# Weight loads of a four-layer decoder trunk: two pairs of row blocks (1 MB) at a time, into one buffer of eight pairs that the remainders overwrite

## The reference

```python
for i in range(DEPTH):                      # 4; x is (1, 256, 2048)
    hn = rmsnorm(x, norm_g[i])
    if kind == 0:   y = diff_attention(hn, da_w_in[j], da_w_out[j], ...)   # w_in 2048 x 8192
    elif kind == 1: y = sliding_window_attention(hn, sw_w_in[j], ...)      # w_in 2048 x 4608
    else:           y = mlstm(hn, ml_w_in[j], ..., ml_w_out[j], ...)       # w_in 2048 x 8208
    x = x + y
return rmsnorm(x, final_g)
# inside each mixer
proj = h @ w_in
...
return (o * silu(g)) @ w_out               # w_out 2048 x 2048
```

## Time and profile before

| | us |
|---|---|
| time, median of 3 runs | 1760.14 |
| lowest and highest | 1760.11, 1761.57 |
| the profiled execution, its own time | 1759.14 |
| its span, first to last instruction | 1757.4 |
| PE busy | 1747.9 |
| DVE busy | 1142.0 |
| ACT busy | 908.9 |

### The profile page before, as it was taken

One profiled execution on the slowest core, in us unless ns is written; L12 is line 12 of the kernel. 1 busy time (PEld: TensorE's weight loads), 2 busy tenths in 40 slices (PEclk: granted clock), 3 DMA queues, 4 the chain that ended last, 5 costly groups with the idle time before them and its releaser, 6 DMA issues.

```text
span 1757.4 us, 25060 instructions
## 1 busy us (share of the span) xinstructions
PE 1747.9 (99%) x8278; PEld 1459.6 (83%) x8278; DVE 1142.0 (65%) x1900; ACT 908.9 (52%) x1420; POOL 38.0 (2%) x99
## 2 busy tenths in 40 slices
PE   9999999999999999999999999999999999999998
PEld 7888888888888888888888888888888888888887
DVE  6766766665658888855656455655666666666655
ACT  7454545454546666655544445444545445454543
POOL 1000000000000000000000000000000000000000
PEclk9999999999999999999999999999999999999999
DMA  8565565555565554556997699855565656556564
GB/s 252 179 188 177 171 188 166 181 174 184 186 189 165 156 154 140 172 179 165 161 165 200 186 162 181 212 173 190 181 184 163 182 178 182 177 179 179 167 215 144
DMA packets 171012, 313.16 MB, mean 178 GB/s; under 512 B 10838, under 2 KB 27804, under 8 KB 170812
## 3 DMA queue, kind: packets, MB, share of 16 engines
q1 hardware_dynamic: 170512, 311.02, 62.9%
q10 hardware_dynamic: 380, 1.08, 0.2%
q0 software_dynamic: 48, 0.13, 0.1%
HBM read 310.10 MB, written 2.10 MB: 178 GB/s over the span
## 4 chain that ended last, share of the span: by engine, by line
PE 98%; issue 1%; DVE 0%; ACT 0%; DMA 0%; SPq 0%; POOLq 0%; POOL 0%; DVEq 0%; ACTq 0%
PE acc L944 30%; PE acc L946 30%; PE acc L945 30%; PE tp L909 4%; PE sc L945 1%; PE sc L946 1%; PE sc L944 1%; PE sc L976 0%; DMA xres<-in_x_dram 0%; PE sc L1030 0%; PE sc L1032 0%; ACT w_hi L881 0%; PE sc L1031 0%; PE sc L1014 0%; PE sc L1013 0%
## 5 line engine op out<-in xcount | busy, mean ns | idle before, releaser
L1755 DVE TENSOR_TENSOR w_lo<-raw,w_hi 128x1024 fp32r<-128x1024 f32 x583 | 708.2, 1223 | 468.1 <-ACT w_hi L881 466.9
L881 ACT ACTIVATE w_hi<-raw 128x1024 fp32r<-128x1024 f32 x583 | 613.4, 1058 | 467.4 <-PE acc L946 415.2
L944 PE MATMUL acc<-w_hi,xt_hi 128*128 128x512 f32 x1824 | 720.5, 395 | 0.0
L946 PE MATMUL acc<-w_hi,xt_lo 128*128 128x512 f32 x1824 | 711.8, 390 | 0.0
L945 PE MATMUL acc<-w_lo,xt_hi 128*128 128x512 f32 x1824 | 710.6, 390 | 0.0
L946 PEld LDWEIGHTS acc<-w_hi,xt_lo 128*128 128x128 f32 x1824 | 342.6, 188 | 73.0
L945 PEld LDWEIGHTS acc<-w_lo,xt_hi 128*128 128x128 f32 x1824 | 343.2, 188 | 65.9
L944 PEld LDWEIGHTS acc<-w_hi,xt_hi 128*128 128x128 f32 x1824 | 342.9, 188 | 65.5
L944 PE MATMUL acc<-w_hi,ot_hi 128*128 128x512 f32 (+1 forms) x520 | 202.7, 390 | 0.0
L946 PE MATMUL acc<-w_hi,ot_lo 128*128 128x512 f32 (+1 forms) x520 | 201.0, 387 | 0.0
L945 PE MATMUL acc<-w_lo,ot_hi 128*128 128x512 f32 (+1 forms) x520 | 200.6, 386 | 0.0
(11 more groups left out here) (286 smaller groups left out, 1136.3 us busy)
## 6 DMA issues: line engine op xcount, KB each, us to landing
raw<-in_da_w_in_dram SPq DMA_DIRECT2D x255, 512.0 KB, 3.8
raw<-in_ml_w_in_dram SPq DMA_DIRECT2D x96, 512.0 KB, 5.4
raw<-in_sw_w_in_dram SPq DMA_DIRECT2D x72, 512.0 KB, 3.8
raw<-in_da_w_out_dram SPq DMA_DIRECT2D x64, 512.0 KB, 4.3
raw<-in_sw_w_out_dram SPq DMA_DIRECT2D x32, 512.0 KB, 4.0
raw<-in_ml_w_in_dram SPq DMA_DIRECT2D x64, 256.0 KB, 4.7
raw<-in_ml_w_out_dram SPq DMA_DIRECT2D x32, 512.0 KB, 4.6
xres<-in_x_dram SPq DMA_DIRECT2D x3, 512.0 KB, 10.0
```

Of the source, the lines that this page charges most:

```text
L881: act.activation(w_hi[:, q:q + 2, :], raw[:, q:q + 2, :], ACT.Copy).then_inc(hi_ready, 1)
L944: pe.matmul(out_ap, k_hi, m_hi, start=start, stop=False)
L946: return pe.matmul(out_ap, k_lo, m_hi, start=False, stop=stop)
L1755: dve.tensor_tensor(w_lo[:, q:q + 2, :], raw[:, q:q + 2, :], w_hi[:, q:q + 2, :].bitcast(F32), ALU.subtract).then_inc(lo_ready, 1)
```

## The change

Raw weights and remainders share one buffer of 16 chunks, a whole job. `raw` is placed, its place is given back, and `w_lo` is put at the same address: DVE's subtraction now writes over the raw weights that it reads. `w_hi` stays a ring of four pairs. In SBUF this takes as much as before: 16 + 8 chunks in place of three times 8.

SP loads two pairs (four chunks, 1 MB) with one transfer. It waits for PE instead of DVE: the transfer for pairs P and P+1 goes out when PE is through with pair P-7, the second of the two pairs that lie in the same place. For the "ml" job q and k there are two transfers of 512 KB, one for each column stripe, as before two of 256 KB. ACT waits for a landing at even pairs only. In the first job the weights still come by single pairs, now with no wait for any slot, and the parts of `x` stand elsewhere among them.

```diff
@@ buffers @@
-        raw = sb("raw", [P, RING, JW])
-        w_hi, w_lo = sb("w_hi", [P, RING, JW], F32R), sb("w_lo", [P, RING, JW], F32R)
+
+        with ExitStack() as place:
+            raw = place.enter_context(nc.sbuf_tensor("raw", [P, KC, JW], F32))
+        w_lo = sb("w_lo", [P, KC, JW], F32R)
+        w_hi = sb("w_hi", [P, RING, JW], F32R)
@@ semaphores @@
-        raw_full = [sem(f"raw_full{s}") for s in range(4)]
-        raw_half = [sem(f"raw_half{s}") for s in range(4)]
+        raw_full = [sem(f"raw_full{s}") for s in range(PAIRS)]
+        raw_half = [sem(f"raw_half{s}") for s in range(PAIRS)]
@@ load_first @@
-                    for n in {2: (1,), 4: (2, 3)}.get(p, ()):
-                        load_x(n)
+                    if p in (2, 3, 5):
+                        load_x((p + 1) // 2)
                     if p == LAG:
                         load_small()
-                    s = p % LAG
-                    if p >= LAG:
-                        sp.wait_ge(lo_ready, p + 1 - LAG)
+                    s = p
@@ load_out @@
-                for q in range(len(OUT_ORDER)):
+                for q in range(0, len(OUT_ORDER), 2):
                     n, p = OUT_ORDER[q]
-                    s = q % LAG
-                    sp.wait_ge(lo_ready, PAIRS * OUT0[l] + q + 1 - LAG)
...
+                    assert OUT_ORDER[q + 1] == (n, p + 1)
+                    s = q % PAIRS
+                    sp.wait_ge(pairs_done, PAIRS * (OUT0[l] - 1) + q + 2)
...
@@ load @@
-                for p in range(PAIRS):
-                    s = p % LAG
-                    sp.wait_ge(lo_ready, PAIRS * J + p + 1 - LAG)
-                    rows_of = w[P * 2 * p:P * 2 * p + 2 * P, :].rearrange("(k p) n -> p k n", p=P)
+                for p in range(0, PAIRS, 2):
+                    s = p
+                    sp.wait_ge(pairs_done, PAIRS * J + p + 2 - PAIRS)
+                    rows_of = w[P * 2 * p:P * 2 * p + 4 * P, :].rearrange("(k p) n -> p k n", p=P)
                     if pair_of:
...
-                            sp.dma_start(raw[:, 2 * s:2 * s + 2, half * a:half * a + half],
+                            sp.dma_start(raw[:, 2 * s:2 * s + 4, half * a:half * a + half],
...
-                        sp.dma_start(raw[:, 2 * s:2 * s + 2, :], rows_of[:, :, bass.ds(col, JW)])\
+                        sp.dma_start(raw[:, 2 * s:2 * s + 4, :], rows_of[:, :, bass.ds(col, JW)])\
                           .then_inc(raw_full[s], 16)
@@ ACT, pair @@
-                act.wait_ge(raw_full[p % LAG], 32 * J + 16 * (p // LAG + 1))
-                if w.kind == "ml" and w.phase == "iter" and j == 0:
-                    act.wait_ge(raw_half[p % LAG], i * 32 + 16 * (p // LAG + 1))
+                by_pairs = j0 == 0 and w.first
+                if by_pairs or p % 2 == 0:
+                    act.wait_ge(raw_full[p], 16 * J + 16)
+                    if w.kind == "ml" and w.phase == "iter" and j == 0:
+                        act.wait_ge(raw_half[p], i * 16 + 16)
...
-                    act.activation(w_hi[:, q:q + 2, :], raw[:, q:q + 2, :], ACT.Copy).then_inc(hi_ready, 1)
+                    act.activation(w_hi[:, q:q + 2, :], raw[:, 2 * p:2 * p + 2, :], ACT.Copy).then_inc(hi_ready, 1)
@@ PE, pair @@
-                slot = 2 * (p % LAG)
+                slot, whole = 2 * (p % LAG), 2 * p
...
-                    at = (slot + k - 2 * p) % RING
...
-                    return three(acc[b][t][:], hi[:, k, c], lo[:, k, c], w_hi[:, at, :], w_lo[:, at, :], k == 0, stop)
+                    at, at_lo = (slot + k - 2 * p) % RING, whole + k - 2 * p
...
+                    return three(acc[b][t][:], hi[:, k, c], lo[:, k, c], w_hi[:, at, :], w_lo[:, at_lo, :], k == 0, stop)
@@ DVE, pair @@
-                    dve.tensor_tensor(w_lo[:, q:q + 2, :], raw[:, q:q + 2, :], w_hi[:, q:q + 2, :].bitcast(F32),
+                    two = slice(2 * p, 2 * p + 2)
+                    dve.tensor_tensor(w_lo[:, two, :], raw[:, two, :], w_hi[:, q:q + 2, :].bitcast(F32),
                                       ALU.subtract).then_inc(lo_ready, 1)
```

More of the change, by code:

```diff
@@ L451, in load_out @@
             def load_out(w, l):
-                for q in range(len(OUT_ORDER)):
+                for q in range(0, len(OUT_ORDER), 2):
                     n, p = OUT_ORDER[q]
-                    s = q % LAG
-                    sp.wait_ge(lo_ready, PAIRS * OUT0[l] + q + 1 - LAG)
-                    rows_of = w[P * 2 * p:P * 2 * p + 2 * P, :].rearrange("(k p) n -> p k n", p=P)
-                    sp.dma_start(raw[:, 2 * s:2 * s + 2, :], rows_of[:, :, JW * n:JW * n + JW]).then_inc(raw_full[s], 16)
+                    assert OUT_ORDER[q + 1] == (n, p + 1)
+                    s = q % PAIRS
+                    sp.wait_ge(pairs_done, PAIRS * (OUT0[l] - 1) + q + 2)
+                    rows_of = w[P * 2 * p:P * 2 * p + 4 * P, :].rearrange("(k p) n -> p k n", p=P)
+                    sp.dma_start(raw[:, 2 * s:2 * s + 4, :], rows_of[:, :, JW * n:JW * n + JW]).then_inc(raw_full[s], 16)
                     if l == NL - 1 and q == 2 * PAIRS:
@@ L1177, in pair @@
                             for k in range(KC - RING, KC):
-                                at = (slot + k - 2 * p) % RING
+                                at, at_lo = (slot + k - 2 * p) % RING, whole + k - 2 * p
                                 m = three(acc[1 - b][n][:, 0:S], hi[:, k, P:S], lo[:, k, P:S], w_hi[:, at, cols],
-                                          w_lo[:, at, cols], k == KC - RING, k == KC - 1)
+                                          w_lo[:, at_lo, cols], k == KC - RING, k == KC - 1)
                             m.then_inc(tiles_done, 1)
```

## The result

| | before | changed |
|---|---|---|
| time, median, us | 1760.12 (4 runs) | 1769.28 (4 runs) |
| lowest and highest | 1760.06, 1761.57 | 1768.14, 1773.26 |
| profiled execution, its span | 1759.14, 1757.4 | 1768.14, 1766.4 |

The ratio of the runs is 1.0057, 95% interval 1.0045 to 1.0069. By the medians the changed kernel is slower by 9.2 us, where 2.4 were forecast; that is 0.8 us above the range.

The account below looks back on a forecast made before the run. PE was taken to bound the kernel, busy 1747.9 of 1757.4 us. Stalls of 1.2 + 1.25 + 0 = 2.4 us on the median 1760.14 gave 1762.5 us, range 1759.3 to 1768.5.

Parts of the forecast that it names:

- Nothing to gain: Whole kernel: PE-bound and no PE instruction added or removed, so no gain unless matmuls themselves get faster.
- The second pair of a couple lands when it did: Full weight queue: same bytes in same order, so a couple's second pair lands unchanged, the first with it.
- The first pair is held for one service: Weight loads: a couple's first pair lands one pair's service later, 3.1 us in a full stretch.
- First spot: Pair 36, first "ml" iteration: late landing delays DVE, `gs` and PE's transposes; PE stalls 1.2 us.
- Second spot: Pair 18, third "ml" iteration: copy 2.65 us later delays `k` and the subtraction of pair 19; PE 1.25 us late.
- Third spot: Pair 36, third "ml" iteration: PE already 1.25 us later while landings are not, so 0 counted, at most 1.2 us.
- DVE in place, waits, SP, the first job: Other edits: overwriting at most 0.3 us, first job -0.3 to +1 us, fewer waits and issues; each taken as 0.
- the full stretches get slower: Two full "ml" stretches: new address order may lower the rate; 5% gives 1767, 10% 1776 us; chance 0.24.
- the Trainium skill's advice to batch to at least 1 MiB: Full stretches: if larger transfers save per-transfer cost, both stalls go, 1760.1 us; chance 0.04, within all hidden.

Follow-up runs that it names:

- e9: Changed kernel with two 512 KB transfers per 1 MB couple (256 KB stripes in q and k), ACT held at even pairs until both landed: 1758.42 us, ratio 0.9996.
- e13: Changed kernel, but the "ml" job q and k comes in four 256 KB transfers, pair by pair, ACT held for all four: 1761.96 us, ratio 1.0014.
- e4: Changed kernel with single pairs only in the "ml" job q and k, all other jobs by 1 MB couples: 1759.17 us, ratio 0.9999.
- e10: Kernel before with one edit, x's parts in the first job placed as in the changed kernel: 1758.41 us, ratio 0.9998.
- e11: Changed kernel with single pairs in the "ml" projection, couples elsewhere, and x's parts placed as in the kernel before: 1758.36 us, ratio 0.9997.
- e16: The changed kernel run once more, unaltered, against the kernel before: 1767.05 us, ratio 1.0040.
- e5: Changed kernel, 1 MB transfers, every "ml" iteration reading one fixed block's columns (q and k block 0, v, o and g block 1): 1757.93 us, ratio 0.999.
- e14: Changed kernel, but job q and k comes in four 256 KB transfers, stripe 0 of both pairs first, ACT held for all four: 1763.98 us, ratio 1.0025.

## Why the prediction was wrong

- *Nothing to gain:* right. No kernel that reads the right weights is below 0.9992 of the kernel before, and no interval of those excludes 1 on that side.
- *"The second pair of a couple lands when it did":* this is the step that failed. It rested on a full queue that carries the same bytes in the same order at the same rate. The order is not the same (four row blocks of a stripe before the other stripe), and in that job the rate was lower: the job q and k took 29.8 and 27.7 us for 25.7 and 23.5. Against PE the couple was 2.9 and 2.6 us later (lateness 8.4 and 7.6 for 5.5 and 5.0).
- *The first pair is held for one service:* true, but by itself without price (e9). There the couple is 1.4 and 2.8 us closer to PE than before; what else differs is the shared buffer and the earlier issue, which the prediction credited with keeping the queue full and nothing more. The hold costs once the couple is late as well: e13 against e4 is 2.4 us, though e4 also issues each even pair earlier. The held kernels fit one relation: PE's waits at a spot add up to the lateness less about 4.2 us, to within 0.6 us. The prediction's own 1.2 us at the first spot is close to the 1.3 that it gives for the lateness of before, 5.5.
- *First spot:* the right place and chain, 1.2 us counted, 6.1 measured. The waits are 3.7, where the couple was 2.9 us later against PE than counted; 1.6 are the lower clock behind the stall, which had no term in the sum, and 0.8 are short gaps.
- *Second spot,* 1.25 us counted: nothing, since PE came 4.7 us later to it. *Third spot,* 0 counted, as absorbed: 4.4 us. The stream was slower again and used up the 4.7 us that the first stall had given it.
- *DVE in place, waits, SP, the first job,* 0 each: right (1222 ns; e10, e11).
- *The rivals:* "the full stretches get slower" is nearest to what happened, and its chance was too small, for an argument that only looked at the bytes per packet. Its price, 1767 for 5%, is near the measured times by luck: it spread the loss evenly over the stretches, while the jobs o and g of the third iteration took 2% longer (50.2 us for 49.2), those of the first no longer (50.7 for 51.7), and the job q and k, with the thinnest cover, took 16 and 18% longer. Here the Trainium skill's advice to batch to at least 1 MiB (DMA: Bandwidth & Descriptors, Bandwidth), which the prediction weighed, went the wrong way: 1 MB for 512 KB in the other jobs cost 3.0 us (e9 to e13), and the job q and k was about 2 to 4 us faster by 256 KB in the order of the pairs than by 512 KB. The page's figures are for transfers issued by GpSimd; here SP issues them.
- *The time:* the miss is a small one by the number, and e16, at 1767.05 us, lies inside the range. The mechanism was no better for it: both executions show the same late couple and the same two stalls, so a time inside the range would have been luck.

What stays open: why larger transfers of these stripes are slower. The runs show that the size matters, by the medians the order too, and neither in the columns of e5; which addresses meet in the memory was not tried.

## What to carry to other kernels

Where the DMA engines are full, treat the rate as something that a change of transfer size or order can move, look for the job with the least room before its landing, and multiply the change by that job alone. Price an engine's stall on TensorE with what its clock does afterwards, and keep larger transfers out of stretches where the queue has no gaps; where it had gaps, they brought nothing here either. A load can be made earlier and larger at once and the two cancel: test them apart.

## What the runs showed of the hardware

- The rate of a weight read depended on its columns. With rows 32,832 bytes apart some blocks of 512 columns kept the 16 DMA engines full (share 1.02) at 166 to 174 GB/s, while others met a demand of 166 to 180 GB/s at a share of 0.61 to 0.66. Rotating the blocks moved this with them.
- Of seven stalls of 2.5 to 3.1 us (those of the kernel with 2 MB not counted), six were followed by the lower of TensorE's clock levels (granted clock 0.56 to 0.85 over 5 us, 0.83 over 10 us in e14), and one, the changed kernel's at the third spot, was not (1.00). It cost 1.6 us at the changed kernel's first spot and 2.9 at e16's. Eight stalls of up to 1.0 us were followed by none.
- At a full queue a stripe's transfer of 512 KB took up to 18.1 us from issue to landing; outside "ml", 1 MB took 5.0 to 5.7.
